# Second block's attention with short and long query tiles in turn, and one accumulation group for a pair of heads

## The reference

```python
def nsa_attention(q, k_c, v_c, k_s, v_s, k_w, v_w, gate_logits, ...):
    # kc, vc: 31 compressed keys and values, each from 32 tokens
    ...
        sc = jnp.einsum('bgrqd,bgcd->bgrqc', qb, kc).astype(f32) - slopes * d_c
        p_c = jax.nn.softmax(sc, axis=-1) * (t >= CMP_LEN - 1).astype(f32)[:, None]
        o_c = jnp.einsum('bgrqc,bgcd->bgrqd', p_c, vc)
    ...
        o_s = jnp.einsum('bgrqnk,bgqnkd->bgrqd', p_s, v_sel)
    ...
        o_w = jnp.einsum('bgrqk,bgkd->bgrqd', jax.nn.softmax(sw, axis=-1), vwb)
        return gb[0] * o_c + gb[1] * o_s + gb[2] * o_w
```

## Time and profile before

| what | value |
|---|---|
| median of 3 runs | 1999.46 us (1990.83, 1999.46 and 2000.87) |
| the profiled execution | 1992.1 us, of which the span 1990.0 us |
| PE busy over the span | 1872.8 us (94%) |
| granted TensorE clock, mean of the span | 0.956 of full speed |
| the second block's attention loop, from the first scores of unit c to the end of the last output copy | 1384.55 to 1509.62 us, 125.07 us |
| PE busy in it | 100.09 us |
| DVE, ACT, POOL busy in it | 82.01, 73.07, 3.33 us |

### The profile page before, as it was taken

One profiled execution on the slowest core, in us unless ns is written; L12 is line 12 of the kernel. 1 busy time (PEld: TensorE's weight loads), 2 busy tenths in 40 slices (PEclk: granted clock), 3 DMA queues, 4 the chain that ended last, 5 costly groups with the idle time before them and its releaser, 6 DMA issues. The chain is left out here.

```text
span 1990.0 us, 26010 instructions
## 1 busy us (share of the span) xinstructions
PE 1872.8 (94%) x8878; PEld 1513.5 (76%) x8878; DVE 1021.1 (51%) x1797; ACT 777.2 (39%) x1235; POOL 882.1 (44%) x1158
## 2 busy tenths in 40 slices
PE   6999999999999999999999999997887799999997
PEld 5767788888887866788888878886555588888885
DVE  6667556666654377566666555333763342222223
ACT  3444443333334344443333334554653242222223
POOL 5543445555555532454555553337001325555551
PEclk9999999999998999999999999988887879999998
DMA  6221224444322221233444321213001202322311
GB/s 232 85 85 43 75 80 145 146 143 147 131 73 97 87 83 43 87 104 136 149 137 148 105 84 66 85 43 127 1 1 43 85 0 95 116 84 86 125 42 43
DMA packets 102964, 183.46 MB, mean 92 GB/s; under 512 B 6714, under 2 KB 66668, under 8 KB 100844
## 3 DMA queue, kind: packets, MB, share of 16 engines
q1 hardware_dynamic: 102504, 181.74, 26.6%
q10 hardware_dynamic: 388, 0.79, 0.1%
HBM read 180.42 MB, written 2.10 MB: 92 GB/s over the span
## 5 line engine op out<-in xcount | busy, mean ns | idle before, releaser
L772 POOL TENSOR_TENSOR w_lo<-raw,w_hi 128x256 fp32r<-128x256 f32 (+1 forms) x1148 | 879.2, 799 | 1068.7 <-ACT w_hi L815 1068.4
L1896 PE MATMUL ps<-n_hi,w_hi 128*128 128x512 f32 x1408 | 560.9, 398 | 9.5 <-DVE n_lo L1278 5.5
L1897 PE MATMUL ps<-n_lo,w_hi 128*128 128x512 f32 x1408 | 551.8, 392 | 0.0
L1898 PE MATMUL ps<-n_hi,w_lo 128*128 128x512 f32 x1408 | 551.5, 392 | 0.0
L815 ACT ACTIVATE w_hi<-raw 128x1024 fp32r<-128x1024 f32 (+1 forms) x331 | 310.5, 944 | 322.6 <-PE ps L1898 199.3
L1896 PEld LDWEIGHTS ps<-n_hi,w_hi 128*128 128x128 f32 x1408 | 266.7, 189 | 70.3 <-issue 9.7
L1897 PEld LDWEIGHTS ps<-n_lo,w_hi 128*128 128x128 f32 x1408 | 266.4, 189 | 57.5 <-issue 3.4
L1898 PEld LDWEIGHTS ps<-n_hi,w_lo 128*128 128x128 f32 x1408 | 266.3, 189 | 56.4
L1896 PE MATMUL ps<-x_hi,w_hi 128*128 128x512 f32 x672 | 273.2, 406 | 8.9 <-DVE x_lo L1278 8.9
L1897 PE MATMUL ps<-x_lo,w_hi 128*128 128x512 f32 x672 | 269.1, 400 | 0.0
L1898 PE MATMUL ps<-x_hi,w_lo 128*128 128x512 f32 x672 | 268.8, 400 | 0.0
(11 more groups left out here) (270 smaller groups left out, 1992.2 us busy)
## 6 DMA issues: line engine op xcount, KB each, us to landing
raw<-in_w_up SPq DMA_DIRECT2D x44, 1024.0 KB, 6.9
raw<-in_w_ff SPq DMA_DIRECT2D x32, 1024.0 KB, 6.1
raw<-in_w_in SPq DMA_DIRECT2D x28, 1024.0 KB, 7.3
zb<-in_ada_w SPq DMA_DIRECT2D x16, 1536.0 KB, 8.1
raw<-in_w_down SPq DMA_DIRECT2D x44, 512.0 KB, 4.3
raw<-in_w_out SPq DMA_DIRECT2D x12, 1024.0 KB, 6.7
za<-in_x SPq DMA_DIRECT2D x1, 2048.0 KB, 10.1
raw<-in_cmp_w_k SPq DMA_DIRECT2D x2, 1024.0 KB, 6.7
```

What stands on the lines that cost most here:

```text
L772: last = pool.tensor_tensor(parts[0][:, c], parts[1][:, c], parts[2][:, c], ALU.subtract)
L1896: pe.matmul(out, l_hi, r_hi, start=start, stop=False)
L1897: pe.matmul(out, l_hi, r_lo, start=False, stop=False)
L1898: return pe.matmul(out, l_lo, r_hi, start=False, stop=stop)
```

## The change

The order of a pair's units becomes c, s0, s3, w0, w3, s1, s2, w1, w2. Unit v (mod 9) = 1 is still s0, and unit v (mod 9) = 8 is now w2. Since s0 and s3 now lie ahead of w0 and w3, several query tiles are open in one bank at a time; only the compressed product of query tile 0 starts the group, for each head, and only the products of the pair's last unit stop it.

```diff
@@ attention_units
     units = []
     for hp in range(HEADS2 // 2):
         units.append((hp, "c", 0))
-        for i in range(NT):
-            units += [(hp, "s", i), (hp, "w", i)]
+        for short, long in ((0, NT - 1), (1, NT - 2)):
+            units += [(hp, br, i) for br in ("s", "w") for i in (short, long)]
     return units
@@ build, PE
                         for m in range(2):
                             pe.matmul(outs[m], vcmp[0:NCMP, 64 * g:64 * g + 64], pTc[0:NCMP, m, i * P:(i + 1) * P],
-                                      start=True, stop=False)
+                                      start=(i == 0), stop=False)
                     pe.wait_ge(turn_out, v + 1)
                     for kt in range(i + 1):
                         for m in range(2):
                             last = pe.matmul(outs[m], v2[0 if br == "s" else 1][:, kt, 64 * g:64 * g + 64],
                                              pT2[PV_BEFORE[v] % 2][:, m, kt * P:(kt + 1) * P],
-                                             start=False, stop=(br == "w" and kt == i))
+                                             start=False, stop=(v % 9 == 8 and kt == i))
```

## The result

| | before | changed |
|---|---|---|
| median, 22 runs each | 1995.96 us (1990.64 to 2004.34) | 2003.12 us (1997.34 to 2014.32) |
| ratio | | 1.0033, 95% interval 1.0019 to 1.0046 |
| profiled execution, its span | 1992.1, 1990.0 us | 2000.65, 1998.5 us |

A forecast was written before the change was run, and what follows sets the result against it. No engine is full; a two-step chain of hand-overs between engines bounds attention. Terms 1.7 + 0.8 + 0 + 1.5 = +4.0 us on the mean of 1995.8 gave 1999.8 us, range 1989 to 2010.

The forecast's parts named there:

- The loops, +2.5: Attention pairs two to four: costlier scores-to-scores chains, +1.7 us for the second and third pair, +0.8 for the last.
- The loop of two steps: Scores, maximum, exponentials, copy, transposes, products, then scores two units on; a full-clock pair goes from 26.67 to 27.50 us, +0.83.
- Flags at nothing: Compressed products in attention: 12 fewer group starts cost or save 0 us; nothing waits on a stop.
- Last pair +0.8: Last pair of heads: three costlier loops, then a drain over shorter w2; +0.8 us, ends 0 and +1.7.
- first pair 0: First pair: norm's vector work stands beside the same number of wide units; 0 us, ends -1 and +3.
- The clock, +1.5: PE in pairs two to four: more idle brings more half clock; +1.5 us, ends -5.7 and +5.7.
- the scaling by three for two: PE's clock: three long idles a pair instead of two would cost +2.9 us; half was taken.
- A sign of being wrong: Pairs at 24 us or less, loops beginning at short units, or granted clock under 0.8 in pairs two to four.
- The other signs: Loops 5.8, 7.2, 6.4, 6.3 us; pair 27.5; s0-to-s3 near 1.8; copy releasing transposes after 1 to 2 us idle.
- The work does not balance: Rival denied here: alternating widths average out in attention, waits go, 25 us less, 1971; chance 0.03.
- The clock gave way: Rival: idles ahead of transposes of s0, w0, s1 keep the attention loop at half speed, 2024 us; chance 0.08.
- the change does nothing: Rival: DVE or the scores' hand-over paces the steps; pairs stay at 26.67, time 1996 us; chance 0.03.

The follow-up runs named there:

- idle-filled kernels: Extra identity transposes on PE ahead of waiting transposes, pairs two to four: in the order of before 0.9977, 1993.55 us; in the changed order 0.9993, 1994.59 us.
- flags-only kernels: Order of before with the change's start and stop flags: 1.0008, 1996.46 us.
- turning the couples round: Changed kernel with the long unit first in each couple (c, s3, s0, w3, w0, s2, s1, w2, w1): 1.0095 of before, 2015.2 us.
- the best order without that move: Changed kernel with only the order made c, s2, s3, w3, w2, s0, s1, w1, w0: 0.9978 of before, 1989.16 us.

## Why the prediction was right, and which term was too small

- *Sign and verdict.* Within 0.5%, and a little slower: so it came, +6.6 us for +4.0. On the profiled execution, for which the sum was made, it was +8.5 for +4.0. The loops, +2.5, were right and for the reason given; the rest of the gap is one term, the clock.
- *The loop of two steps.* Right in each step: 5.81, 7.21, 6.36, 6.30 and 1.82 measured for 5.82, 7.21, 6.38, 6.31 and 1.78. The idle-filled kernels put the difference at 0.82 a pair for 0.83. Taking the exponentials out of the loop removed the penalty with the loop.
- *Flags at nothing.* Borne out by the steps of the trace and, within 0.25%, by the time. The starts that went are 24 and not 12, since each query tile had one for each of two heads; at nothing apiece that changes no sum.
- *Last pair +0.8, first pair 0.* Measured +0.81 at full clock, and 32.42 for 32.41. The first pair's reason was weak: of the units beside the norm's vector work two are 384 columns or wider now (w3, s2) and three were before (s2, w2, s3). And its granted clock was 0.79 in place of 0.71, so that two things may have balanced. With the filled and the flags-only kernels, whose first pairs have nothing added, it is 31.76 to 32.41 in the old order and 32.11 and 32.42 in the new; no run here separates a cost of the order there from the clock.
- *The clock, +1.5.* This is the mis-sized term: +6.2 in the profiled execution, just past its upper end of +5.7. It failed twice. The share of half clock was to grow little; by the windows it went from 19.1 us in pairs two to four to 30.7 (twice one less the granted clock, times the length: 13.7, 3.5 and 13.5). And its price was held at 0.30 us for each us, while it was 11.7 / 30.7 = 0.38 in the new order. Three idles of nearly 2 us a pair in place of two of 1.64 and 1.69 did what the scaling by three for two said, +2.9, and more. Halving that because PE works in longer runs between them had no row behind it. The price depends on where the half clock falls: from s0 to s3, where PE has no wait to hide it in, 3.25 us at half clock cost 1.43, or 0.44 for each us.
- *A sign of being wrong that came.* The granted clock of pairs two to four was to lie between 0.85 and 0.95, and under 0.8 would be wrong. It was 0.79, 0.94 and 0.83. The other signs came as forecast, but for the idles: up to 2.13 us ahead of s0's transposes and only 0.89 ahead of w1's, for 1 to 2.
- *The rule of the Trainium skill* that short idles between groups of matmuls make the clock go to and fro (TensorE: Matmul & The Clock Gate, the section on a second failure mode) pointed at this term. The traces agree: with the idle filled the granted clock of pairs two to four was 1.00, where it had been 0.88 to 0.91. A single idle decides little, though: in the third pair of the changed kernel the clock stayed full behind two of 1.84 us and fell behind the one of 1.96 between them.
- *The rivals.* The work does not balance: pairs did not fall to 24 us, and turning the couples round cost 19 us. The clock gave way only in part, 31 of 101 us and not throughout, so 2024 was not reached. That the change does nothing is out: the steps changed each as said.
- *The range*, 1989 to 2010, held the median. Single runs reached 2014.32. It was wide enough because it starts from the lowest and highest single executions; the clock term by itself left its bounds.
- *The copies.* Behind the exponentials of c and s0 now stand the copies of w1 and w2, and not of s2 and w2 as the part on the change has it. The loops were added up with the right copies.

## What to carry to other kernels

Where engines pass a unit round in a fixed order, walk the chain once from the timeline and close it against the distance of two starts; then see how many steps it spans and which units it meets. Here a mix of long and short with the loop's own period cost time, and cost nothing once the loop was gone; other mixes of short and long in turn were not tried. Better than reordering the units is to find the instruction that stands in a queue ahead of the one that is waited for: here a copy moved ahead of two exponentials won 15.6 us, where the best order without that move won 4.4 us.

## What the runs showed that was not expected

Extra matmuls in idle time are not merely free. In before, pairs two to four took 5.5 us less with 26, 31 and 36 extra transposes: the clock stayed at 2.4 GHz.

The runs of one and the same kernel spread over 10 us and more (before: 1990.64 to 2004.34), and the profiled executions suggest that a good part of that is not in the attention at all. The stretch ahead of it, between the last sums of the final norm (L1922) and the first transposes of the compressed branch (L2290), has the same instructions in all kernels. It took 158.10 and 156.60 us in the profiled executions of before and of the change, and 165.40 in both of two experiments, the flags alone and the idle filled in the order of before. All ten profiled executions have either 156.6 to 158.8 us or 165.4 to 165.6, five each. Whether one kernel changes from one to the other between its executions was not looked at, since each was profiled once. These windows of the three kernels, before, flags alone and idle filled, differ in the granted clock:

```profile
1212.50:1370.60 158.10, 152.68 (x803) 131.94 (x802) 65.18 (x79) 79.20 (x100) 63.98 (x87) 0.91 0.21 70
```

```profile
1215.90:1381.30 165.40, 160.07 (x802) 137.57 (x802) 65.17 (x79) 79.23 (x100) 62.78 (x86) 0.87 0.19 64
```

```profile
1215.40:1380.80 165.40, 160.03 (x804) 137.53 (x803) 64.60 (x79) 79.29 (x100) 62.93 (x86) 0.87 0.19 64
```

So the time of this kernel can move by more than the change is worth, and the lengths of its stages, each with its granted clock, say more than the total.
